# Keys of the second mixer turned once and swapped between partition halves; values projected as features and transposed

## The chip, the cores and the metric

The kernel runs on one core of one Trainium2 chip. The metric is the device time of one execution in microseconds. Three executions of the kernel before took 2218.27, 2221.05 and 2222.43 us; their median, 2221.05 us, is the time before.

## The reference

A network of two blocks on one sequence of 256 positions and width 1024, each block two layers deep, all in fp32. The change lies in the mixer of the second block. There the normalised activations `h` are multiplied by a wide matrix `w_in`, and its columns are split into queries, keys and values of several attention branches, a convolution branch and a pooling branch:

```python
proj = h @ w_in[l]
a_q, a_kv, a_gate, d_q, d_kv, b_in, c_in = jnp.split(proj, splits, axis=-1)
qa = a_q.reshape(bsz, seq, NSA_KV, NSA_R, HEAD_DIM)
kv = a_kv.reshape(bsz, seq, 3, 2, NSA_KV, HEAD_DIM)      # compressed, selected, window
k_cmp = nsa_compress(kv[:, :, 0, 0], ...)                # not rotated
o_slc = nsa_selected_attention(qa_rot, apply_rope(kv[:, :, 1, 0], cos, sin), kv[:, :, 1, 1], sel)
o_win = banded_attention(qa_rot, apply_rope(kv[:, :, 2, 0], cos, sin), kv[:, :, 2, 1], NSA_WINDOW, None)
kvd = d_kv.reshape(bsz, seq, 2, SWA_KV, HEAD_DIM)
o_d = banded_attention(qd, apply_rope(kvd[:, :, 0], cos, sin), kvd[:, :, 1], SWA_WINDOW, swa_sinks[l])

def apply_rope(x, cos, sin):
    x1, x2 = xf[..., : HEAD_DIM // 2], xf[..., HEAD_DIM // 2:]
    return jnp.concatenate([x1 * c - x2 * s, x2 * c + x1 * s], axis=-1)
```

So three branches (selected, window, and the sliding one called d) have keys that are rotated and values that are not. Each has two key heads of 64 features, that is 128 key columns and 128 value columns of `w_in`, and eight query heads, four to each key head.

## The kernel before

Everything is one program for one core. Activations lie with features on partitions and the 256 positions along the free axis. A product with a weight matrix goes in **units** of 1 MB of weights (256 output columns). SyncE loads a unit into one of three slots of a ring (`raw`), ScalarE rounds it to a high part `whi` (`split_hi`, L1287), VectorE computes the low part `wlo` (`split_lo`, L1823), and TensorE multiplies: each product of fp32 accuracy is three matmuls, high by high, high by low, low by high (`mm3`, L615 to L617). A unit is split two units before it is used; ScalarE may overwrite a slot when TensorE is done with the unit that lay there, and SyncE may load into it when its low part is made.

A normal unit is two halves of 128 output columns, each 8 chunks of the depth times three matmuls with 256 moving columns (`project`), 48 matmuls in all. TensorE writes the result into a PSUM bank, and VectorE takes it from there, times the reciprocal norm (`take`).

`mixer2` walks over units 0 to 47 of a layer on TensorE, ScalarE, VectorE and SyncE alike; each engine has its own loop over the same unit numbers, and semaphores tie them. The order inside a unit is written out by hand. The units that matter here are 7, 8 and 9, the **key units** (`K_UNITS`: selected, window, d). The first half of such a unit is the keys (features on partitions). The second half is the values, with positions on partitions as the product with the probabilities needs them: `project_tokens` makes `h` the stationary operand and the weights the moving one, for each of two tiles of 128 positions 8 chunks times three matmuls with 128 moving columns (L702 to L704), again 48.

After unit 8, 9 and 10 TensorE does the **turn** of the keys of the unit before (`TURNS`, kind "k"). The keys of two heads lie on partitions 0 to 63 and 64 to 127. The score products of a pair of query heads use partition half 0 for the one and half 1 for the other, so each key head must stand on both halves. For this the kernel multiplies with a duplicating matrix `dup[g]` and with `rotdup[g]` (duplicate and rotate), four fp32 matmuls of 256 columns (L1054). Each fp32 matmul of this kind leaves two rows in the trace, so a turn has x8. VectorE then makes `kd = dup*cos + rotdup*sin` in three operations of 512 columns (L2302, L2303, L2305). The turn after unit 7 is that of the compressed branch ("cmp"), also four matmuls with `dup`, with eight small VectorE additions (L2314) behind it. The turns after units 2, 3, 11 and 12 rotate queries (L1049).

VectorE's list in the units around this, per unit i: convolution taps (L2436, 5 to 8 of 256 columns), the rest of the turn of unit i-1, the low split for unit i+2, and `take(i)`. From unit 13 on it also has softmax work, at unit 14 the pooling windows (L2407 to L2422), and at unit 16 the low part of the pooled product (L2522). TensorE's product for the pooling (`pool_mix`, L1163) stands behind unit 14; the first transposes of probabilities (L1081) stand behind unit 16. The first score product (`scores(0)`, L1071) stands behind unit 13.

## Time and profile before

| | us |
|---|---|
| median of three executions | 2221.05 |
| the profiled execution | 2222.18 |
| its span in the trace | 2220.4 |
| TensorE busy in the span | 2159.3 (97%) |
| VectorE busy | 1497.8 (67%) |
| ScalarE busy | 1099.7 (50%) |
| mean granted TensorE clock | 0.988 of full |

The span is what the trace covers; 1.8 us of the profiled execution lie outside it. Matmuls overlap, so the duration of one (about 280 ns) is much longer than the distance to the next (0.11 to 0.12 us), and it is the distance that counts in a row of them. The two mixers of the second block lie at about 1120 to 1460 us and 1660 to 1990 us, the two feed-forward stages behind them at about 1480 to 1650 and 2030 to 2200 us.

### The profile page before, as it was taken

How to read it: one execution, taken by the hardware profiler on the slowest of the kernel's cores; microseconds unless marked ns; L12 is line 12 of the kernel's file. 1: busy time of each engine (PE TensorE's matmuls, PEld its weight loads, DVE VectorE, ACT ScalarE, POOL GpSimd, SP SyncE). 2: the span in 40 equal slices, each digit the busy share in tenths (PEclk: the TensorE clock that was granted, in tenths of full speed). 3: DMA queues.
4: the chain of work that ended last, by engine and by line, in shares of the span. 5: the costliest groups of instructions: out<-in, count | busy, mean ns of one | idle time of the engine just before them, and what ended most of it. 6: DMA issues, size and time to landing. Idle time of an engine off the chain costs nothing.

```text
span 2220.4 us, 40876 instructions
## 1 busy us (share of the span) xinstructions
PE 2159.3 (97%) x17966; PEld 2079.9 (94%) x17966; DVE 1497.8 (67%) x1814; ACT 1099.7 (50%) x1336; POOL 127.1 (6%) x116
## 2 busy tenths in 40 slices
PE   8999999999999999999999799999999989999998
PEld 8999999999999999999999698999999879899998
DVE  5556757554655675765568996667766898666775
ACT  5444465444544436544442567455554365655553
POOL 0001000000100100000000000001000000001000
PEclk9999999999999999999999899999999989999999
DMA  7555444555555454455563444346554344354552
GB/s 258 193 187 167 157 143 162 190 190 189 172 186 190 163 164 143 162 190 192 189 191 118 140 142 144 123 163 205 195 180 134 117 146 150 121 171 143 187 184 76
DMA packets 285044, 367.26 MB, mean 165 GB/s; under 512 B 10002, under 2 KB 257730, under 8 KB 284610
## 3 DMA queue, kind: packets, MB, share of 16 engines
q1 hardware_dynamic: 281138, 361.01, 49.3%
q10 hardware_dynamic: 3728, 3.62, 0.5%
q8 instruction: 142, 2.33, 0.4%
q14 instruction: 36, 0.29, 0.0%
HBM read 363.56 MB, written 1.05 MB: 164 GB/s over the span
## 4 chain that ended last, share of the span: by engine, by line
PE 86%; DVE 9%; ACT 3%; issue 1%; DMA 1%; POOL 0%; ACTq 0%; SPq 0%; DVEq 0%
PE ps L615 25%; PE ps L617 25%; PE ps L616 25%; DVE wlo L1823 2%; ACT whi L1287 2%; PE ps L702 1%; PE ps L703 1%; PE ps L704 1%; PE ps L663 1%; DVE sq L2436 1%; PE ps L1054 1%; PE ps L1071 1%; PE ps L1102 1%; PE ps L1081 1%; DVE arena L2112 0%
## 5 line engine op out<-in xcount | busy, mean ns | idle before, releaser
L615 PE MATMUL ps<-hhi,whi 128*128 128x256 f32 x3808 | 1087.7, 286 | 15.5 <-DVE hlo L1829 4.7
L1823 DVE TENSOR_TENSOR wlo<-raw,whi 128x2048 fp32r<-128x2048 f32 (+1 forms) x347 | 781.7, 2254 | 426.6 <-ACT whi L1287 426.5
L616 PE MATMUL ps<-hlo,whi 128*128 128x256 f32 x3808 | 1062.9, 279 | 0.0
L617 PE MATMUL ps<-hhi,wlo 128*128 128x256 f32 x3808 | 1062.7, 279 | 0.0
L1287 ACT ACTIVATE whi<-raw 128x2048 fp32r<-128x2048 f32 (+1 forms) x347 | 652.9, 1884 | 700.6 <-PE ps L617 611.7
L615 PEld LDWEIGHTS ps<-hhi,whi 128*128 128x128 f32 x3808 | 717.4, 188 | 34.3 <-issue 12.9
L616 PEld LDWEIGHTS ps<-hlo,whi 128*128 128x128 f32 x3808 | 717.0, 188 | 6.5 <-issue 6.0
L617 PEld LDWEIGHTS ps<-hhi,wlo 128*128 128x128 f32 x3808 | 720.9, 189 | 0.2
L615 PE MATMUL ps<-hidhi,whi 128*128 128x256 f32 x1056 | 295.5, 280 | 0.3 <-DVE hidlo L2193 0.3
L617 PE MATMUL ps<-hidhi,wlo 128*128 128x256 f32 x1056 | 294.7, 279 | 0.0
L616 PE MATMUL ps<-hidlo,whi 128*128 128x256 f32 x1056 | 294.7, 279 | 0.0
L617 PEld LDWEIGHTS ps<-hidhi,wlo 128*128 128x128 f32 x1056 | 200.4, 190 | 0.0
L615 PEld LDWEIGHTS ps<-hidhi,whi 128*128 128x128 f32 x1056 | 198.5, 188 | 0.9 <-DVE hidlo L2193 0.5
L616 PEld LDWEIGHTS ps<-hidlo,whi 128*128 128x128 f32 x1056 | 198.6, 188 | 0.0
L1365 ACT ACTIVATE arena<-arena 128x512 f32<-128x512 f32 x44 | 27.8, 633 | 176.5 <-DVE arena L1858 176.4
L615 PE MATMUL ps<-brhi,whi 128*128 128x256 f32 x320 | 92.0, 287 | 7.4 <-DVE brlo L2544 6.6
L2436 DVE SCALAR_TENSOR_TENSOR sq<-arena,par,sq 128x256 f32<-128x256 f32 x240 | 98.1, 476 | 0.0
L1780 POOL TENSOR_TENSOR arena<-arena,rstd 128x512 f32<-128x512 f32 x44 | 57.1, 1298 | 629.5 <-ACT arena L1365 603.6
L616 PE MATMUL ps<-brlo,whi 128*128 128x256 f32 x320 | 90.6, 283 | 0.0
L617 PE MATMUL ps<-brhi,wlo 128*128 128x256 f32 x320 | 90.5, 283 | 0.0
L2188 DVE SCALAR_TENSOR_TENSOR arena<-arena,par 128x256 f32<-128x256 f32 x176 | 73.6, 479 | 1.5 <-ACT arena L1549 1.3
L615 PEld LDWEIGHTS ps<-brhi,whi 128*128 128x128 f32 x320 | 62.0, 194 | 9.2 <-issue 7.7
(288 smaller groups left out, 2108.7 us busy)
## 6 DMA issues: line engine op xcount, KB each, us to landing
raw<-in_ffn_w_up SPq DMA_DIRECT2D x88, 1024.0 KB, 5.1
raw<-in_w_in SPq DMA_DIRECT2D x68, 1024.0 KB, 5.2
raw<-in_ffn_w_down SPq DMA_DIRECT2D x66, 1024.0 KB, 4.8
raw<-in_ffn_w_gate SPq DMA_DIRECT2D x43, 1024.0 KB, 5.2
raw<-in_w_gate SPq DMA_DIRECT2D x32, 1024.0 KB, 5.4
raw<-in_w_branch SPq DMA_DIRECT2D x16, 1024.0 KB, 4.9
raw<-in_nsa_cmp_w SPq DMA_DIRECT2D x8, 1024.0 KB, 5.5
raw<-in_w_out SPq DMA_DIRECT2D x6, 1024.0 KB, 4.8
```

The costliest lines, as they stand in the source:

```text
L615: pe.matmul(o, w_hi, m_hi, start=start, stop=False, skip_group_check=True)
L616: pe.matmul(o, w_hi, m_lo, start=False, stop=False, skip_group_check=True)
L617: return pe.matmul(o, w_lo, m_hi, start=False, stop=stop, skip_group_check=True)
L663: last = pe.matmul(bank(2, n * t, n), src[:, chunk, t * P:(t + 1) * P], w, start=first and t == 0, stop=final, skip_group_check=True)
L702: pe.matmul(o[:, t, :], hhi[:, k, tok], whi[:, slot, c:c + n], start=(k == 0), stop=False)
L703: pe.matmul(o[:, t, :], hlo[:, k, tok], whi[:, slot, c:c + n], start=False, stop=False)
L1287: act.activation(whi[:, slot, 0:n], raw[:, slot, 0:n], ACT.Copy).then_inc(hi_ready[slot], 1)
L1365: act.activation(act_out, gate_sb, ACT.Silu).then_inc(act_done, 1)
L1780: pool.tensor_tensor(scaled.rearrange("p (c t) -> p c t", c=2), act_out.rearrange("p (c t) -> p c t", c=2), rstd_over(2), ALU.mult).then_i ...
L1823: dve.tensor_tensor(wlo[:, slot, 0:n], raw[:, slot, 0:n], whi[:, slot, 0:n].bitcast(F32), ALU.subtract) \
L2188: dve.scalar_tensor_tensor(conv2[:, w, c, :], pad2[:, w, c, tap:tap + SEQ], par_col(ch + tap * FCH), conv2[:, w, c, :], ALU.mult, ALU.add) ...
L2436: dve.scalar_tensor_tensor(conv_acc[:, c, :], x, w, conv_acc[:, c, :], ALU.mult, ALU.add) \
```

## The change

In the key units the values are now projected like everything else, features on partitions, and taken together with the keys by one VectorE operation into `ktv`. In the turn TensorE transposes the values of the unit (two transposes of 128 columns into bank 3) and rotates the keys once, by one fp32 matmul of 256 columns into bank 4. ScalarE copies the transposed values out of PSUM to `vt`. VectorE computes `keys*cos + rotated*sin` once, for 256 columns, into `kd[:, k, 0]`. Two DMAs, issued by ScalarE, copy partitions 64 to 127 to 0 to 63 of `kd[:, k, 1]` and the other way round. The score product picks copy 0 or 1 according to whether the key head already lies on the half that the query uses. The compressed branch is as it was. The table of constants of the second block loses `rotdup` (256 of 2178 columns). Three semaphores of the first normalisation are merged into others with the same waits.

```diff
-C2_AT, C2_N = layout([("cos", SEQ), ("sin", SEQ), ("rot", P), ("dup", 2 * P), ("rotdup", 2 * P),
+C2_AT, C2_N = layout([("cos", SEQ), ("sin", SEQ), ("rot", P), ("dup", 2 * P),
...
-        ktmp = view(m2["s"][:, 0:3 * SEQ], k=3, t=SEQ)
-        cmp_kv = view(m2["s"][:, 3 * SEQ:5 * SEQ], v=2, t=SEQ)
+        ktv = view(m2["s"], k=3, v=2, t=SEQ)
+        cmp_kv = ktv[:, 2, :, :]
...
 # TensorE, turn
+                    elif kind == "k":
+                        if k:
+                            pe.wait_ge(v_taken, l * 3 + k)
+                        for t in range(TT):
+                            last = pe.transpose(bank(3, t * P, P), ktv[:, k, 1, t * P:(t + 1) * P], ident)
+                        last.then_inc(v_turned, 1)
+                        last = pe.matmul(bank(4, 0, SEQ), rot2, ktv[:, k, 0, :], start=True, stop=True)
                     else:
-                        for b, m, src in ((3, dup, ktmp[:, k, :]), (4, rotdup, ktmp[:, k, :])) if kind == "k" else \
-                                ((3, dup, cmp_kv[:, 0, :]), (4, dup, cmp_kv[:, 1, :])):
+                        for v in range(2):
                             for g in range(KVH):
-                                last = pe.matmul(bank(b, g * SEQ, SEQ), m[:, g, :], src, start=True, stop=True)
+                                last = pe.matmul(bank(3 + v, g * SEQ, SEQ), dup[:, g, :], cmp_kv[:, v, :], start=True, stop=True)
...
 # TensorE, scores
                     if j == 0:
                         pe.wait_ge(rope2_done, (l + 1) * len(ROPES) - 1)
+                        pe.wait_ge(v_taken, (l + 1) * 3)
+                        pe.wait_ge(k_swapped, (l + 1) * 3 * 32)
...
-                            k = kd[lane, kind, 2 * c // GRP, 0:keys]
+                            k = kd[lane, kind, int(i != 2 * c // GRP), 0:keys]
...
 # TensorE, second half of every unit
-                            if i in K_UNITS:
-                                last = project_tokens(slot, P, P, UC, bank(b, SEQ, SEQ).rearrange("p (t n) -> p t n", t=TT))
-                            else:
-                                last = project(slot, 1, bank(b, SEQ, SEQ))
-                            last.then_inc(used[slot], 1)
+                            project(slot, 1, bank(b, SEQ, SEQ)).then_inc(used[slot], 1)
...
 # ScalarE, per unit
+                    for unit, kind, k in TURNS:
+                        if kind == "k" and unit + 1 == i:
+                            act.wait_ge(v_turned, l * 3 + k + 1)
+                            act.activation(vt[:, k, :, :], bank(3, 0, TT * P).rearrange("p (t n) -> p t n", t=TT), ACT.Copy) \
+                                .then_inc(v_taken, 1)
+                        if kind == "k" and unit + 2 == i:
+                            act.wait_ge(rope2_done, l * len(ROPES) + ROPE_OF_K[k] + 1)
+                            for half in range(2):
+                                act.dma_start(kd[half * DH:(half + 1) * DH, k, 1, :], kd[(1 - half) * DH:(2 - half) * DH, k, 0, :]) \
+                                    .then_inc(k_swapped, 16)
...
 # VectorE, take
-                    if i in K_UNITS:
-                        k = K_UNITS[i]
-                        dve.tensor_tensor(ktmp[:, k, :], bank(bank2_of(f), 0, SEQ), rstd_b, ALU.mult)
-                        dve.tensor_tensor(vt[:, k, :, :], bank(bank2_of(f), SEQ, SEQ).rearrange("p (t n) -> p t n", t=TT),
-                                          rstd_t.unsqueeze(2).broadcast_to([P, TT, P]), ALU.mult).then_inc(taken2, 1)
-                        return
...
+                    elif i in K_UNITS:
+                        dst = ktv[:, K_UNITS[i], :, :]
...
 # VectorE, turn
-                        dve.tensor_tensor(kd[:, k, :, :], two(bank(3)), cos2, ALU.mult)
-                        dve.tensor_tensor(ropes2, two(bank(4)), sin2, ALU.mult).then_inc(rot2_taken, 1)
+                        same, part = kd[:, k, 0, :], ropes2[:, 0, :]
+                        dve.tensor_tensor(same, ktv[:, k, 0, :], cos2[:, 0, :], ALU.mult)
+                        dve.tensor_tensor(part, bank(4, 0, SEQ), sin2[:, 0, :], ALU.mult).then_inc(rot2_taken, 1)
                         dve.wait_ge(rot2_taken, r + 1)
-                        dve.tensor_tensor(kd[:, k, :, :], kd[:, k, :, :], ropes2, ALU.add).then_inc(rope2_done, 1)
+                        dve.tensor_tensor(same, same, part, ALU.add).then_inc(rope2_done, 1)
```

How instructions stand on TensorE where unit 8 of the first layer ends and its turn follows, before (`arena` holds all buffers of a mixer; `consts` the table; `ps` is PSUM):

```order
9424 L702 MATMUL ps<-whi,hhi 128x128
9425 L703 MATMUL ps<-whi,hlo 128x128
9426 L704 MATMUL ps<-wlo,hhi 128x128
9427 L1054 MATMUL ps<-arena,consts 128x256 x4
9428 L615 MATMUL ps<-hhi,whi 128x256
9429 L616 MATMUL ps<-hlo,whi 128x256
```

And the same place after the change (its line numbers are 3 to 8 higher):

```order
9376 L618 MATMUL ps<-hhi,whi 128x256
9377 L619 MATMUL ps<-hlo,whi 128x256
9378 L620 MATMUL ps<-hhi,wlo 128x256
9379 L1057 MATMUL ps<-ident,arena 128x128 x2
9380 L1059 MATMUL ps<-arena,consts 128x256
9381 L618 MATMUL ps<-hhi,whi 128x256
```

The matmuls of 128 columns are gone from the unit's end, and the four fp32 products of the turn have become two transposes and one product. Nothing else of TensorE has moved: the unit, the turn and the next unit follow one another as they did.

ScalarE in units 8 to 15 of the first layer, before:

```order
416 L1287 ACTIVATE whi<-raw 128x2048 x3
417 L1677 ACTIVATE hidhi<-gates 128x480 x2
418 L1287 ACTIVATE whi<-raw 128x2048 x2
419 L1287 ACTIVATE whi<-raw 128x192
420 L1287 ACTIVATE whi<-raw 128x2048 x3
```

After:

```order
417 L1684 ACTIVATE arena<-ps 128x256
418 L1694 ACTIVATE hidhi<-gates 128x480 x2
419 L1294 ACTIVATE whi<-raw 128x2048
420 L1689 DMA arena<-arena 64x256 x2
421 L1684 ACTIVATE arena<-ps 128x256
422 L1294 ACTIVATE whi<-raw 128x2048
423 L1689 DMA arena<-arena 64x256 x2
424 L1684 ACTIVATE arena<-ps 128x256
425 L1294 ACTIVATE whi<-raw 128x192
426 L1689 DMA arena<-arena 64x256 x2
```

The three value copies and the three pairs of swap DMAs stand between the high splits, each behind the split of its own unit. The last pair stands behind the small split (192 columns) for unit 14 and ahead of the split for unit 15.

## Rows read from the trace of the kernel before

**Rows 1.** Units 7 to 12: busy us of PE, PEld, DVE, ACT, POOL; clock, DMA.

```profile
1170.00:1219.00 49.00, 49.00 (x392) 47.45 (x391) 40.42 (x71) 10.64 (x9) 0.00 (x0) 1.00 0.35 108
```

**Rows 2.** Waits of TensorE: total us, times, the longest.

```profile
PE ps L1163 <- DVE gates L2422: 16.9, 2, 8.7
PE ps L1081 <- DVE brlo L2522: 8.8, 2, 5.0
PE ps L615 <- DMA consts<-const_tables: 2.1, 1, 2.1
```

**Rows 3.** The chain that ended last, 1130 to 1330 us: start, us, what.

```profile
1212.21 0.86 PE ps L1049 x2
1218.76 0.69 DVE gates L2281
...
1262.96 0.66 PE ps L1081 x6
```

**Rows 4.** Timeline of TensorE, units 8 and 9: start, us, instruction, x how many.

```profile
1182.01 0.22 PE L702 MATMUL ps<-whi,hhi 128*128 128x128 f32 x1
...
1187.32 1.94 PE L1054 MATMUL ps<-arena,consts 128*128 128x256 f32 x8
1188.91 0.47 PE L615 MATMUL ps<-hhi,whi 128*128 128x256 f32 x1
1189.21 0.28 PE L616 MATMUL ps<-hlo,whi 128*128 128x256 f32 x1
...
1191.92 0.22 PE L702 MATMUL ps<-whi,hhi 128*128 128x128 f32 x1
```

**Rows 5.** The same view of two stretches of the feed-forward stages.

```profile
1520.00:1540.00 20.00, 20.00 (x179) 20.00 (x178) 14.41 (x16) 10.61 (x11) 2.44 (x2) 1.00 0.60 202
2080.00:2100.00 20.00, 20.00 (x173) 20.00 (x172) 13.21 (x16) 11.18 (x11) 2.58 (x2) 1.00 0.62 208
```

**Rows 6.** Timeline of VectorE, units 7 to 12, first layer.

```profile
1173.42 2.28 DVE L1823 TENSOR_TENSOR wlo<-raw,whi 128x2048 fp32r<-128x2048 f32 x1
1177.60 0.42 DVE L2250 TENSOR_TENSOR arena<-ps,rstd 128x256 f32<-128x256 f32 x1 [1.90 <-PE ps L704]
...
1183.27 2.29 DVE L1823 TENSOR_TENSOR wlo<-raw,whi 128x2048 fp32r<-128x2048 f32 x1
...
1197.43 0.42 DVE L2250 TENSOR_TENSOR arena<-ps,rstd 128x256 f32<-128x256 f32 x1 [3.06 <-PE ps L704]
...
1200.08 0.68 DVE L2302 TENSOR_TENSOR arena<-ps,consts 128x512 f32<-128x512 f32 x1
...
1202.01 2.28 DVE L1823 TENSOR_TENSOR wlo<-raw,whi 128x2048 fp32r<-128x2048 f32 x1
1204.21 1.22 DVE L2321 TENSOR_TENSOR hidlo<-gates,hidhi 128x480 fp32r<-128x480 f32 x2
...
1212.24 0.69 DVE L2283 SCALAR_TENSOR_TENSOR arena<-ps,rstd 128x512 f32<-128x512 f32 x1
...
1217.22 0.35 DVE L1823 TENSOR_TENSOR wlo<-raw,whi 128x192 fp32r<-128x192 f32 x1
1218.76 0.69 DVE L2281 TENSOR_TENSOR gates<-ps,rstd 128x512 f32<-128x512 f32 x1 [1.18 <-PE ps L617]
```

**Rows 7.** Timeline of VectorE, the same units, second layer.

```profile
1717.04 2.28 DVE L1823 TENSOR_TENSOR wlo<-raw,whi 128x2048 fp32r<-128x2048 f32 x1
...
1761.82 0.69 DVE L2281 TENSOR_TENSOR gates<-ps,rstd 128x512 f32<-128x512 f32 x1 [0.99 <-PE ps L617]
```

**Rows 8.** Timelines: ScalarE's queue issuing three DMAs; TensorE's first scores in the first layer.

```profile
1114.73 1.69 ACTq L1640 DMA_DIRECT2D arena<-in_nsa_cmp_w  x3
...
1225.16 0.92 PE L1071 MATMUL ps<-arena 64*128 64x256 f32 x8
```

**Rows 9.** DMA issues: queue, count, KB each, median us to landing.

```profile
consts<-const_tables ACTq DMA_DIRECT2D x1, 1089.0 KB, 7.4
...
arena<-in_nsa_cmp_w ACTq DMA_DIRECT2D x6, 64.0 KB, 4.5
```

More of the change, by code:

```diff
@@ L191, in shape_consts @@
     half = (r[:, None] // DH) == np.arange(2)[None, :]
-    c2 = np.concatenate([cos, sin, rot, *dup, *(x @ rot for x in dup), *causal, *window, cmpadd, cmp01, blockdiag, inv, half], 1)
+    c2 = np.concatenate([cos, sin, rot, *dup, *causal, *window, cmpadd, cmp01, blockdiag, inv, half], 1)
     return (np.eye(P, dtype=np.float32), np.ascontiguousarray(c1, np.float32), np.ascontiguousarray(c2, np.float32))
@@ L343, in hybrid_network @@
         rot2 = table(C2_AT, "rot", P)
-        dup, rotdup = (view(table(C2_AT, x, 2 * P), g=KVH, n=P) for x in ("dup", "rotdup"))
+        dup = view(table(C2_AT, "dup", 2 * P), g=KVH, n=P)
         causal, window = (table(C2_AT, x, 3 * P).unsqueeze(1).broadcast_to([P, 2, 3 * P]) for x in ("causal", "window"))
@@ L398, in hybrid_network @@
         x_updated = sem("x_updated")
-        first_sq, first_root, first_rec, first_diag, first_wide, first_kept = (
-            sem(n) for n in ("first_sq", "first_root", "first_rec", "first_diag", "first_wide", "first_kept"))
+        first_sq, first_diag, first_wide, first_kept = (
+            sem(n) for n in ("first_sq", "first_diag", "first_wide", "first_kept"))
         h_hi, h_ready = sem("h_hi"), sem("h_ready")
@@ L422, in hybrid_network @@
             "kcvb_done kcvb_taken sc_scored hid_turned sc_step sc_exp sc_den sc_pt ptc_taken s2_done s2_taken mn2_step p2_done "
-            "den2_step rec2_done p2_normed t2_done pt2_taken pv2_done ob2_hi ob2_ready cg_on c_ready conv_step "
+            "rec2_done p2_normed t2_done pt2_taken pv2_done ob2_hi ob2_ready cg_on c_ready conv_step "
             "ln_mean ln_cent ln_sqd ln_var ln_stdd ln_step silu_done ga_raw ga_tanh ga_on pads pool_step pooled pool_mm "
             "pool_hi pool_lo gates_on br_done gated2 y2_done y2_hi y2_ready").split())
+        v_turned, v_taken = sem("v_turned"), sem("v_taken")
+        k_swapped = sem("k_swapped")
         block = ctx.enter_context(nc.Block())
@@ L808, in first_rstd @@
             def first_rstd():
-                pe.wait_ge(first_diag, 1)
+                pe.wait_ge(first_diag, 2)
                 pe.matmul(bank(3, 0, SEQ), ones, diag.rearrange("p t n -> p (t n)"), start=True, stop=True).then_inc(first_wide, 1)
@@ L1422, in first_norm @@
                 act.wait_ge(first_sq, 2)
[L1423 removed]
+                act.activation(col_std[:, 0:TT], col_tmp[:, 0:TT], ACT.Sqrt, scale=1.0 / D, bias=eps_col).then_inc(first_sq, 1)
             def turned_par():
@@ L1932, in first_norm @@
                 low(7)
-                dve.wait_ge(first_root, 1)
-                dve.reciprocal(col_rec[:, 0:TT], col_std[:, 0:TT]).then_inc(first_rec, 1)
-                dve.wait_ge(first_rec, 1)
+                dve.wait_ge(first_sq, 3)
+                dve.reciprocal(col_rec[:, 0:TT], col_std[:, 0:TT]).then_inc(first_diag, 1)
+                dve.wait_ge(first_diag, 1)
                 widen(col_rec[:, 0:TT], diag).then_inc(first_diag, 1)
```

3 lines of the change are left out of this document (1 added, 2 removed).

## The prediction

> **What bounds the kernel now.** I read the busy times first, for the whole span (TensorE 97%, in the table above) and for the stretch of units 7 to 12: TensorE is busy for 49.00 of 49 us there, VectorE for 40.42, ScalarE for 10.64 [rows 1]. Where a kernel is bound like that, a matmul taken out is worth its distance to the next one, unless TensorE then only waits longer further on. So the second view is the list of TensorE's waits [rows 2]: few, and the two large ones (16.9 and 8.8 us over both layers, two waits each) stand in the second mixer, shortly behind the units that the change touches. The third view, the chain of waits in order of time, tells which engine sets the pace there. Up to 1212 us its long pieces are TensorE's own, the turns among them; at 1218.76, with VectorE's take of unit 12, it goes over to VectorE, and only behind the wait at L1081 do TensorE's turns and transposes come back into it [rows 3]. So units 7 to 12 are TensorE's, units 13 to 16 VectorE's. The change saves TensorE time just ahead of a stretch that VectorE sets. What it is worth depends on how early VectorE can reach the take of unit 12. For that I read VectorE's timeline, with the idle time ahead of a row and what ended it in brackets.
>
> **The values.** In unit 8 the 48 matmuls of 128 columns run from 1182.01 to 1187.32, 5.31 us, 0.111 us each [rows 4]. Half the columns do not cost half the time: 256 columns cost 0.118 us: from 1189.21, the second matmul of unit 9, to its second half at 1191.92 there are 23, 2.71 us. The change puts 24 matmuls of 256 columns there: 24 x 0.118 = 2.83 us. Saved per key unit 2.48 us. The Trainium skill (TensorE: Matmul & The Clock Gate, Back-to-back issue gap) gives N/2.4 + 2.5 ns for an isolated warm matmul, 109 ns for 256 columns, and about 81 ns for a pair of weight load and 128 columns; by it the unit would save only 48 x 0.081 - 24 x 0.109 = 1.3 us, and the time would come out 7 us higher over the six units. The rows have 111 ns for the 128 columns, so I go by them.
>
> **The turn.** Before, eight rows of L1054 take 1.59 us to the start of the next unit at 1188.91, 0.20 us each, and the second matmul of that unit starts 0.30 instead of 0.12 us later: 1.77 us [rows 4]. After: two transposes, at the 0.11 us of six in 0.66 [rows 3], 0.22 us; one fp32 product, two rows of 0.20; the same 0.18 us of change back: 0.80 us. Saved 0.97 us. Together 3.45 us per key unit, 10.3 us for three, if nothing holds TensorE up.
>
> **Can VectorE follow?** A list of VectorE's work after the change, from the row of the low split at 1173.42, which ends 2.20 us later, at 1175.6 (consecutive starts, as at 1202.01 and 1204.21). The take of unit 7, which waited for TensorE, stood at 1177.60; TensorE is now 2.5 us earlier, so 1175.1, and the take of unit 7 starts at once. From there:
> - to the take of unit 8: 1177.60 to 1183.27 plus a split of 2.20, 7.87 us (the two takes of 256 become one of 512; gain counted as nothing);
> - to that of unit 9: take and taps 2.65 (1197.43 to 1200.08), turn, split 2.20. The turn is 1.93 before (1200.08 to 1202.01); each of its three operations goes from 512 to 256 columns, 0.68 to 0.42 us: 1.93 - 0.78 = 1.15. Sum 6.0;
> - to that of unit 10: 6.0 and the 1.2 of L2321, 7.2; to that of unit 11: 6.0;
> - to that of unit 12: 1212.24 to 1217.22 plus the small split 0.35, 5.3.
>
> Sum 32.4 us: VectorE is ready at 1208.0. TensorE is done with unit 12 at 1218.76 - 10.3 = 1208.4 [rows 6]. VectorE arrives 0.4 us ahead; the first layer gets its 10.3 us, with no idle time of VectorE left. Second layer: 1717.04 + 2.20 + 32.4 = 1751.6 against 1761.82 before [rows 7]; here VectorE is last by a hair and the gain is 10.2 us. In between, TensorE needs the take of the unit before last for its bank and that of the last for the turn, each some 5 us ahead of need. From the take of unit 12 on, VectorE's chain is as long as before, and all behind it moves up by what the take moved up. The two large waits keep their size.
>
> **What is added.** Three copies of 256 columns and six DMA issues per layer on ScalarE, the issues 0.56 us each (1.69 for three, [rows 8]). ScalarE is busy for 10.64 of 49 us there [rows 1]; 0.4 and 1.1 us more per unit lie in its idle time. The last swap waits for VectorE's turn in unit 11 (1196.7 + 2.65 + 1.15 = 1200.5) and for the small split behind unit 11's end (1212.2 - 10.3 = 1201.9 [rows 3], plus 0.4), is issued by 1203.4 and lands, by the 4.5 us of the 64 KB loads [rows 9], at 1208. The first scores come at 1225.16 - 10.3 = 1214.9 [rows 8]. With 7 us of slack it costs nothing; beyond 11.5 us from issue to landing the excess would be on the path. The Trainium skill (DMA: Bandwidth & Descriptors, Rules for kernel authors) says that two transfers to disjoint partition halves serialise, which speaks against the pair. Even twice the row's 4.5 us fits.
>
> **The table.** TensorE waits 2.1 us for the second table [rows 2], 1089 KB in 7.4 us [rows 9]. 128 KB less is 0.87 us if all of the 7.4 scales, and 0.36 by the slope from the 64 KB row (2.9 us for 1025 KB). I take 0.6, bounds 0 (something else late by then) and 0.9. The merged semaphores keep their waits: nothing.
>
> **Sum.** 10.3 + 10.2 + 0.6 = 21.1 us. The profiled execution took 2222.18 us: 2201.1. It is 1.1 us above the median of 2221.05, so the forecast is 2200.0 us.
>
> **An unknown of another kind.** At full granted clock (1.00 in both rows) the same projections run at two paces: 179 matmuls in 20 us in the feed-forward stage of the first layer, 173 in that of the second [rows 5], 3.5%. Nothing in the work differs, so the pace seems to depend on how the engines happen to fall into step behind some pause. The change shifts all that follows, so each later stretch may fall the other way. One feed-forward stage of some 150 us is worth 5 us; one stage was fast and one slow, so I expect 0, with some 6 us to each side.
>
> **Rivals.**
> *VectorE does not get narrower.* If 256 columns out of SBUF and PSUM cost the turn as much as 512 (bound from above: 1.93 us), three turns per layer cost 2.3 us more and VectorE is at unit 12 at 1210.3 and 1753.9: gains 8.5 and 7.9, time 2222.2 - 17.0 - 1.1 = 2204; with each link of its list 0.3 us slower by waits on TensorE, 2207. For: it has no slack left. Against: the row of a 256-column take shows 0.42. Chance 10%.
> *The gain is only a longer wait.* If VectorE set the pace already from unit 7, TensorE would arrive early at L1163 and wait 10 us more: 2221. For: the wait there is the largest. Against: VectorE idles 1.90, 3.06 and 1.18 us in units 7 to 12, each time for TensorE [rows 6]. All that stays is its own shortening, 3 us per layer at most, partly. Chance 4%, between 2215 and 2221.
> *Slower: the swap sets the scores.* The first score product waits for all six DMAs of the layer. It decides from the point at which the last lands after 1214.9, and costs more than the change saves when it lands after 1225.2, 22 us from its issue, with TensorE idle at L1071 and VectorE's softmax behind it. At 30 us it would be 8 us late in each layer: 2221 + 16 = 2237. Against: 4.5 us in the row of the same size, queue nearly empty there. The other way to the same place is a fault of the order, ScalarE held by the wait for the turn while TensorE needs a split; by the times above that wait is always over when it is reached. Chance 3%.
>
> **How the numbers follow.** Forecast 83%, at 2200 with its own range 2193 to 2208 (pace +-6, VectorE's list +-1.5); first rival 10%, near 2205, also mostly inside; second 4%; third 3%. A difference under 0.2% (4.4 us) can't be told from none. So faster 93%, same 4%, slower 3%. Range 2193 to 2208.
>
> **What would show it.** TensorE: no matmuls of 128 columns in units 7 to 9; from the end of unit 8's last projection to the second matmul of unit 9 about 0.9 us. TensorE's busy time down by about 20 us, its waits at L1163 and L1081 as before (some 17 and 9). VectorE: its take of unit 12 near 1208 and 1751 less the table's part, idle time ahead of it under 1 us. The swap landing before the scores, no wait for it. Wrong would be: a new wait at the scores or at the first turn, a wait at L1163 longer by more than 2 us, or VectorE's take of unit 12 above 1210.

## The result, and the profile after

| | before | changed |
|---|---|---|
| median, us (executions) | 2219.83 (4) | 2192.95 (4) |
| lowest and highest, us | 2218.27, 2222.43 | 2189.15, 2200.51 |
| the profiled execution, its span | 2222.18, 2220.4 | 2200.51, 2198.7 |
| TensorE busy in the span, us | 2159.3 | 2136.5 |
| mean granted clock | 0.988 | 0.986 |

The ratio is 0.9878, with a 95% interval from 0.9849 to 0.9907. The forecast was 2200.0 with a range from 2193 to 2208: the median lies 7 us below the forecast, just outside the range, while the profiled execution took 2200.51 us. Only the profiled one of the four executions has a trace. So there are two questions: did the change do what the steps said, and where do the other 7 us come from?

First the stretch that was changed. The windows view of units 7 to 12 in the changed kernel (start:end, total, then busy us and number of instructions of PE, PEld, DVE, ACT, POOL, then clock, DMA share, GB/s), to be held against [rows 1]:

```profile
1164.00:1202.00 38.00, 38.00 (x310) 36.68 (x309) 37.60 (x68) 12.03 (x12) 0.00 (x0) 1.00 0.49 150
```

The same units take 38 instead of 49 us. TensorE has some 80 instructions fewer. VectorE, busy for 40.4 of 49 us before, is now busy for 37.6 of 38. Its timeline, units 6 to 12, against [rows 6] (start, us, instruction; an idle time before a row would stand in brackets):

```profile
1163.58 0.69 DVE L2294 TENSOR_TENSOR arena<-ps,rstd 128x512 f32<-128x512 f32 x1 [1.35 <-PE ps L620]
...
1169.73 0.68 DVE L2294 TENSOR_TENSOR arena<-ps,rstd 128x512 f32<-128x512 f32 x1
...
1177.65 0.69 DVE L2294 TENSOR_TENSOR arena<-ps,rstd 128x512 f32<-128x512 f32 x1
1178.26 2.06 DVE L2450 SCALAR_TENSOR_TENSOR sq<-arena,par,sq 128x256 f32<-128x256 f32 x5
1180.23 0.41 DVE L2316 TENSOR_TENSOR arena<-arena,consts 128x256 f32<-128x256 f32 x1
1180.57 0.41 DVE L2317 TENSOR_TENSOR arena<-ps,consts 128x256 f32<-128x256 f32 x1
1181.02 0.42 DVE L2319 TENSOR_TENSOR arena<-arena 128x256 f32<-128x256 f32 x1
1181.36 2.29 DVE L1840 TENSOR_TENSOR wlo<-raw,whi 128x2048 fp32r<-128x2048 f32 x1
...
1201.75 0.69 DVE L2294 TENSOR_TENSOR gates<-ps,rstd 128x512 f32<-128x512 f32 x1
```

From the take of unit 6 to that of unit 12 it is 1201.75 - 1163.58 = 38.17 us; before it was 1218.76 - 1169.47 = 49.29. The first layer gained 11.1 us. In the second layer the two takes stand at 1699.51 and 1737.69, 38.18 us, against 48.73 (1713.09 to 1761.82): 10.6 us. No row after the first has an idle time ahead of it, and the three operations of the turn, of 256 columns each, take 1181.36 - 1180.23 = 1.13 us.

TensorE's timeline at the turn behind unit 8, against [rows 4]:

```profile
1182.42 0.28 PE L620 MATMUL ps<-hhi,wlo 128*128 128x256 f32 x1
1182.53 0.38 PE L1057 MATMUL ps<-ident,arena 128*128 128x128 f32 x2
1182.75 0.60 PE L1059 MATMUL ps<-arena,consts 128*128 128x256 f32 x2
...
1188.65 0.38 PE L1057 MATMUL ps<-ident,arena 128*128 128x128 f32 x2
...
1200.96 0.28 PE L620 MATMUL ps<-hhi,wlo 128*128 128x256 f32 x1
```

One unit with its turn is 1188.65 - 1182.53 = 6.12 us long. The two transposes take 0.22 us to the start of the key rotation. The last row is the end of unit 12: TensorE is done with it at 1201.24, and VectorE takes it at 1201.75, without idle time ahead. So VectorE is the last by 0.5 us. The waits of TensorE, against [rows 2] (what for, total us, times, the longest):

```profile
PE ps L1174 <- DVE gates L2436: 18.0, 2, 9.1
PE ps L1092 <- DVE brlo L2536: 9.0, 2, 4.5
...
PE ps L618 <- DMA consts<-const_tables: 1.7, 1, 1.7
```

They are the waits of before, 16.9, 8.8 and 2.1 us there. The swap, from the list of DMA issues (KB each, median us to landing) and the timelines of ScalarE's queue and of TensorE, against [rows 8, 9]:

```profile
consts<-const_tables ACTq DMA_DIRECT2D x1, 961.0 KB, 7.0
arena<-arena ACTq DMA_DIRECT2D x12, 64.0 KB, 2.0
```

```profile
1195.05 1.12 ACTq L1689 DMA_DIRECT2D arena<-arena  x2
...
1207.49 0.92 PE L1082 MATMUL ps<-arena 64*128 64x256 f32 x8
```

A pair is issued in 1.12 us, and each copy lands 2.0 us behind its issue (the median of twelve; one took 4.4), here by 1198.2 at the latest; the first scores stand at 1207.49, with no wait.

Now the pace. The windows of 20 us in the five long feed-forward stretches behind the first one (columns: total, PE busy and number of matmuls, clock, DMA share, GB/s), of the profiled execution of the changed kernel:

```profile
440.00:460.00 20.00, 20.00 (x172) 1.00 0.56 177
620.00:640.00 20.00, 20.00 (x179) 1.00 0.58 184
1000.00:1020.00 20.00, 20.00 (x178) 1.00 0.64 210
1520.00:1540.00 20.00, 20.00 (x172) 1.00 0.58 189
2060.00:2080.00 20.00, 20.00 (x172) 1.00 0.51 172
```

Both paces of [rows 5] are there, 172 and 179 matmuls in 20 us, at a granted clock of 1.00. From the distances between the starts of projections in the trace: they are 113.3 ns at the fast pace and 117.8 ns at the slow one (4.4 ns apart, unrounded), and nothing between. A stretch of 1340 takes 151.8 or 157.8 us. Before, the five were slow, slow, fast, fast, slow; here slow, fast, fast, slow, slow. The two profiled executions so have the same number of matmuls at the slow pace, some 8000 each, and the 21.7 us between their spans are the change at equal pace.

### The profile page after: what moved, and what is told of

Same layout as the page of the kernel before. It is cut to its first block, busy times and chain, and to the rows that moved or that the text cites. A ratio compares the mean times of both kernels' runs of the same rounds, so it can differ in the third digit from the quotient of the medians.

```text
span 2198.7 us, 40554 instructions
## 1 busy us (share of the span) xinstructions
PE 2136.5 (97%) x17798; PEld 2058.5 (94%) x17798; DVE 1491.7 (68%) x1808; ACT 1100.5 (50%) x1342; POOL 127.1 (6%) x116
## 4 chain that ended last, share of the span: by engine, by line
PE 83%; DVE 12%; ACT 3%; issue 1%; DMA 1%; POOL 0%; SPq 0%; ACTq 0%; DVEq 0%
PE ps L618 25%; PE ps L620 24%; PE ps L619 24%; DVE wlo L1840 3%; DVE sq L2450 2%; ACT whi L1294 2%; PE ps L666 1%; PE ps L705 1%; PE ps L707 1%; PE ps L706 1%; PE ps L1082 1%; PE ps L1092 1%; PE ps L1113 1%; DVE arena L2129 0%; PE ps L877 0%
## 5 line engine op out<-in xcount | busy, mean ns | idle before, releaser
L618 PE MATMUL ps<-hhi,whi 128*128 128x256 f32 x3856 | 1099.8, 285 | 16.4 <-DVE hlo L1846 5.7
L619 PE MATMUL ps<-hlo,whi 128*128 128x256 f32 x3856 | 1075.4, 279 | 0.0
L620 PE MATMUL ps<-hhi,wlo 128*128 128x256 f32 x3856 | 1075.3, 279 | 0.0
L618 PEld LDWEIGHTS ps<-hhi,whi 128*128 128x128 f32 x3856 | 725.3, 188 | 35.3 <-issue 12.6
L619 PEld LDWEIGHTS ps<-hlo,whi 128*128 128x128 f32 x3856 | 726.8, 188 | 6.5 <-issue 6.0
```

Source lines behind the costliest of these rows:

```text
L618: pe.matmul(o, w_hi, m_hi, start=start, stop=False, skip_group_check=True)
L619: pe.matmul(o, w_hi, m_lo, start=False, stop=False, skip_group_check=True)
L620: return pe.matmul(o, w_lo, m_hi, start=False, stop=stop, skip_group_check=True)
```

## The experiments

Times are medians, with the lowest and the highest in brackets; kernels of one group ran on the same chip with the kernel before. The first group was to tell whether the 7 us come from the change or from the pace.

**The changed kernel again, and its parts.** The first is the changed kernel, unchanged. The second has the values of the change, and the keys rotated as before. The third has the keys of the change and the values as before. The fourth has the whole change but the table in its old size.

> The changed kernel once more, unchanged, beside the kernel before. Between VectorE's take of unit 6 and its take of unit 12 the profiles show 49.3 and 48.7 us before and 38.2 and 38.2 us after, 21.7 us less in both layers together. The first series of times says 27 us less. Theory A (the change is worth what its stretch shows, about 21 to 22 us, and the rest is at which of the two paces the long stretches happen to run): the ratio over more runs moves up towards 0.990, single runs of the changed kernel spread over 10 us, and its span follows the number of matmuls at the slow pace. Theory B (the change also saves some 5 us elsewhere, every time): the ratio stays at 0.988 or below, and a second profile shows the 5 us in one place.

> Only the values are projected as features and transposed (into bank 6); the keys are duplicated and rotated by four products as before, no swap. By the forecast's terms each key unit saves 2.5 us for the projection and pays 0.2 for two transposes: 6.9 us per layer between the takes of units 6 and 12, 13.8 us in all, ratio 0.994. Theory B has no other number for it unless the excess belongs to the values: then 0.9915.

```diff
-                        last = pe.matmul(bank(4, 0, SEQ), rot2, ktv[:, k, 0, :], start=True, stop=True)
+                        for b, m in ((3, dup), (4, rotdup)):
+                            for g in range(KVH):
+                                last = pe.matmul(bank(b, g * SEQ, SEQ), m[:, g, :], ktv[:, k, 0, :], start=True, stop=True)
```

> Only the keys: rotated once, swapped by DMA; the values are projected with positions on partitions as before. The turn goes from 1.77 to about 0.5 us: 3.8 us per layer between the takes of units 6 and 12, 7.6 us in all, and 0.5 for the smaller table, ratio 0.996. With theory B and the excess in the keys or the swap: 0.994.

```diff
-                            project(slot, 1, bank(b, SEQ, SEQ)).then_inc(used[slot], 1)
+                            if i in K_UNITS:
+                                last = project_tokens(slot, P, P, UC, bank(b, SEQ, SEQ).rearrange("p (t n) -> p t n", t=TT))
```

> The changed kernel with the table of constants at its old size (the 256 columns of rotdup are loaded and not used). TensorE's wait for the table goes from 1.7 us back to 2.1 us: 0.4 us slower than the changed kernel if the pace falls alike. Theory B with the excess in the table: 5 us slower, ratio 0.990 where the changed kernel beside it has 0.988.

```diff
-C2_AT, C2_N = layout([("cos", SEQ), ("sin", SEQ), ("rot", P), ("dup", 2 * P),
+C2_AT, C2_N = layout([("cos", SEQ), ("sin", SEQ), ("rot", P), ("dup", 2 * P), ("rotdup", 2 * P),
```

| | us | ratio, 95% interval | take of unit 6 to 12, both layers |
|---|---|---|---|
| before | 2214.00 (2199.71 to 2228.46, 31) | | 49.29, 48.73 |
| changed, again | 2194.94 (2186.18 to 2201.39, 9) | 0.9913 (0.9880 to 0.9946) | 38.17, 38.18 |
| values alone | 2200.85 (2190.97 to 2202.91, 10) | 0.9941 (0.9916 to 0.9967) | 42.16, 41.38 |
| keys alone | 2208.92 (2198.87 to 2213.85, 10) | 0.9986 (0.9959 to 1.0012) | 44.86, 44.86 |
| old table | 2191.33 (2181.72 to 2200.34, 9) | 0.9905 (0.9875 to 0.9935) | 38.18, 38.18 |

The kernel before, which in three executions had spread over 4 us, spreads over 29 us in 31. That alone takes the meaning from a gap of 7 us between medians of four. Over the larger number the gain is 19.1 us, not 26.9. In whole times the keys alone can't be told from no change. In the stretch itself the parts can be told apart to half a microsecond: the values give 7.1 and 7.4 us (by the forecast's terms, less the two transposes, (2.48 - 0.22) x 3 = 6.8), the keys 4.4 and 3.9 (the turn without the transposes, (0.97 + 0.22) x 3 = 3.6), and together 11.6 and 11.2, against 11.1 and 10.6 for the two at once: they add up, less what VectorE takes back. The half microsecond between the layers is the pace again: of the 49.29 us before, 203 projections ran at the slow pace, of the 48.73 us 72, and 131 x 4.4 ns = 0.58 us. The changed kernel's 38.17 to 38.18 us, set by VectorE, don't move with it. The table can't be seen in the times (2191.33 with the old, 2194.94 with the new); its wait is 1.8 to 2.1 us in the four profiles with 1089 KB, and 1.0 to 2.2 in the twelve with 961 KB.

The windows of the changed kernel's second profiled execution:

```profile
440.00:460.00 20.00, 20.00 (x172) 1.00 0.61 198
620.00:640.00 20.00, 20.00 (x173) 1.00 0.59 183
1000.00:1020.00 20.00, 20.00 (x179) 1.00 0.57 180
1520.00:1540.00 20.00, 20.00 (x172) 1.00 0.54 177
2060.00:2080.00 20.00, 20.00 (x179) 1.00 0.58 190
```

The second stretch was fast in the first execution and is slow here, the fifth the other way round, with the same instructions. The pace is no property of the kernel. It varies in the five long stretches; of the two shorter ones at the start (26 to 102 us and 107 to 200 us) the first was fast and the second slow in all ten profiles without a product at their start. To compare single executions I take 4.4 ns off the span for each matmul at the slow pace ("corrected span"): 2185.2 us before, 2163.5 and 2161.4 in the two executions after, 21.7 and 23.8 us apart.

**Is VectorE the last?** One more VectorE product of 512 columns behind each key turn.

> The changed kernel with one more VectorE product of 512 columns (about 0.60 us, result unused) behind each of the three key turns of a layer. Theory A (VectorE is the last to arrive at the take of unit 12, with no idle time left from unit 7 on): each of the three is paid in full, 1.8 us per layer, VectorE's take of unit 6 to that of unit 12 takes 38.2 + 1.8 = 40.0 us in both layers, and the span corrected for the pace (span less 4.4 ns for each matmul run at the slow pace) is 3.6 us above the 2161 to 2163 of the changed kernel. Theory B (TensorE still sets these units and VectorE has slack): the distance stays at 38.2 us, below 38.6, and the corrected span within 1 us. The uncorrected time can move by 5 us either way by the pace alone in both theories.

```diff
                         dve.tensor_tensor(same, same, part, ALU.add).then_inc(rope2_done, 1)
+                        dve.tensor_tensor(spare, ktv[:, k, :, :], cos2, ALU.mult)
```

2194.90 us (2190.51 to 2205.99, 5). The takes of units 6 and 12 on VectorE:

```profile
1168.09 0.69 DVE L2294 TENSOR_TENSOR arena<-ps,rstd 128x512 f32<-128x512 f32 x1 [1.14 <-PE ps L620]
...
1208.05 0.68 DVE L2294 TENSOR_TENSOR gates<-ps,rstd 128x512 f32<-128x512 f32 x1
```

39.96 us, and 39.97 (1701.98 to 1741.95) in the second layer: 1.8 us more, each product paid in full. So units 7 to 12 have changed hands, from TensorE to VectorE, and with this change the place gives no more unless VectorE loses work too. The other half of the expectation was not met: the corrected span is 2163.4 us, 0 to 2 us and not 3.6 above the changed kernel's, and so the 3.6 us are seen in the stretch alone.

**Single small instructions between the projections.** Where two executions of one kernel differ, something short must decide. The stretches differ from their surroundings by what passes TensorE between projections, so I put seven kinds of small instruction there.

> The changed kernel with single small TensorE instructions (a product of 1, 64, 512 and 192 columns in bf16, one of 1 and one of 128 columns in fp32, one transpose; results unused) between the projections of units 3, 4, 5, 10, 6, 8 and 9 of the feed-forward stages behind the first. Theory A (the pace is a phase between weight loads and matmuls that is kept until something else than a projection passes TensorE): at some of the places the distance of the following matmuls changes from 117.8 to 113.3 ns or back, always at the same kind of instruction, and it never changes where there is none. Theory B (the pace is given by memory or by something outside of the order of instructions): the pace of each stage stays what it was at its start, through all seven. The instructions themselves cost about 1 us per stage.

```diff
+                    if p == 3 and f:
+                        pe.matmul(bank(5 - odd, 0, 1), zeros[:, 0:P], zeros[:, 0:1], start=True, stop=True, skip_group_check=True)
...
+                    if p == 8 and f:
+                        pe.matmul(bank(5 - odd, 0, P), ones, ones, start=True, stop=True, skip_group_check=True)
```

2196.92 us (one execution). Windows of 10 us in the first of the five stretches, one behind each instruction:

```profile
415.00:425.00 10.00, 10.00 (x87) 1.00 0.51 158
431.00:441.00 10.00, 10.00 (x87) 1.00 0.38 118
448.00:458.00 10.00, 10.00 (x91) 1.00 0.38 123
465.00:475.00 10.00, 10.00 (x90) 1.00 0.45 139
482.00:492.00 10.00, 10.00 (x90) 1.00 0.45 151
513.00:523.00 10.00, 10.00 (x88) 1.00 0.43 145
530.00:540.00 10.00, 10.00 (x87) 1.00 0.45 150
550.00:560.00 10.00, 10.00 (x91) 1.00 0.61 190
```

The first row lies ahead of all seven and the others follow in the order of the expectation's kinds: 1 column, 64, 512 bf16; 1, 128 fp32; transpose; 192 bf16. Slow is 87 or 88, fast 90 or 91. The other four stretches give the same from the second instruction on:

| stretch from | start | 1 | 64 | 512 | 1 fp32 | 128 fp32 | transpose | 192 |
|---|---|---|---|---|---|---|---|---|
| 411 us | slow | slow | fast | fast | fast | slow | slow | fast |
| 598 | fast | slow | fast | fast | fast | slow | slow | fast |
| 963 | slow | fast | fast | fast | fast | slow | slow | fast |
| 1489 | fast | slow | fast | fast | fast | slow | slow | fast |
| 2022 | fast | slow | fast | fast | fast | slow | slow | fast |

The pace changes only at the instructions, and three of them decide it in 5 of 5 stretches: 64 and 192 columns set the fast one, 128 in fp32 the slow one. One column leaves it to chance (it changed the pace in four of five, three times to slow). All this is one execution, each kind at one place of a stretch. The 64 columns, at which the first stretch turns from slow to fast, in TensorE's timeline:

```profile
444.47 0.28 PE L620 MATMUL ps<-hidhi,wlo 128*128 128x256 f32 x1
444.59 0.20 PE L762 MATMUL ps<-zeros 128*128 128x64 bf16 x1
444.63 0.36 PE L618 MATMUL ps<-hhi,whi 128*128 128x256 f32 x1
```

**Fewer waits behind unit 12, and the swap late.** Two experiments on the waits that the change left.

> The changed kernel with ten of VectorE's 124 convolution taps per layer moved: the six of unit 13 and four of the eight of unit 15 go to units 21, 22, 23, 25 and 27. Theory A (from the take of unit 12 on, VectorE's chain sets the time of the pooled product, L1174, and of the probabilities' transposes): ten taps of 0.41 us are 4.1 us off VectorE's chain; TensorE's wait for VectorE at L1174 (9.0 us per layer) and the one at L1092 (4.5) fall by 4 us together per layer, and the corrected span falls by up to 8 us, provided that VectorE isn't late in units 21 to 27. Theory B (the later taps make VectorE late there): waits of TensorE for VectorE's takes or splits come up in units 22 to 28 and the corrected span falls by under 2 us or rises.

```diff
-CONV_TAPS = {7: 6, 8: 5, 9: 5, 10: 5, 11: 5, 12: 6, 13: 6, 15: 8, 16: 8, 17: 8, 18: 8, 19: 6, 20: 6, 21: 6, 22: 6, 23: 5, 24: 7,
-             25: 4, 26: 7, 27: 7}
+CONV_TAPS = {7: 6, 8: 5, 9: 5, 10: 5, 11: 5, 12: 6, 15: 4, 16: 8, 17: 8, 18: 8, 19: 6, 20: 6, 21: 8, 22: 8, 23: 7, 24: 7,
+             25: 7, 26: 7, 27: 8}
```

2196.47 us (2184.13 to 2202.44, 6). The waits:

```profile
PE ps L1174 <- DVE gates L2436: 15.6, 2, 7.8
...
PE ps L1092 <- DVE brlo L2536: 6.6, 2, 3.3
PE ps L1167 <- DVE arena L2409: 3.4, 2, 1.7
```

27.0 us of waits became 22.2 and one of 1.6 became 3.4, so 3 us are left of the 8 at most; corrected span 2157.5. (In the changed kernel's second execution the 27.0 were 28.6, so a good microsecond of this is scatter.) The whole time doesn't show it: this execution had 8843 matmuls at the slow pace, against 7209.

> The changed kernel with all six swaps of a layer issued in ScalarE's turn of unit 14, about 12 us later than the last is issued now. Theory A (landing is 2.0 us behind the issue and the first scores, at 1207.5 us in the first layer, need all six): issue of six takes 3.4 us from about 1207.6, the last lands near 1213, TensorE waits some 5 us at the first scores; the part of it that VectorE's softmax passes on is 2 to 5 us per layer, so the corrected span rises by 4 to 10 us. Theory B (the swaps have more slack than that because VectorE is the last there anyway): TensorE's wait at the scores appears, but the wait at the probabilities' transposes falls by the same amount and the corrected span rises by under 2 us.

```diff
-                        if kind == "k" and unit + 2 == i:
+                        if kind == "k" and i == 14:
```

2210.62 us (2204.81 to 2218.51, 10). The issue on ScalarE's queue, the scores on TensorE, and the list of DMA issues:

```profile
1208.28 3.75 ACTq L1689 DMA_DIRECT2D arena<-arena  x6
...
1216.42 1.19 PE L1082 MATMUL ps<-arena 64*128 64x256 f32 x3 [8.26 <-DMA arena<-arena]
```

```profile
arena<-arena ACTq DMA_DIRECT2D x12, 64.0 KB, 4.9
```

The third rival's mechanism is real: once the swaps land late, TensorE waits at the scores and all behind it moves (the pooled product 8.6 us, 1228.72 against 1220.13 with unit 12 taken at the same time; 8.1 us in the second layer, counted from the take of unit 12). Both theories priced it too low. Six in a row land 4.9 us behind their issue in the median, not 2.0 as in pairs, the last 1216.4 - 1212.0 = 4.4 us behind the end of the issues; and nothing is made up for: 15.7 us over the changed kernel's 2194.94 (another chip), and as much over the wide-turn version's 2194.90 on the same chip, as the third rival's rule of one for one has it (8 us late in each layer, 16 us).

**Setting the pace.** One product of 192 columns behind the wide product that starts each long feed-forward stretch (7 places in the trace, not the 8 of the expectations), in the changed kernel and in the one before; with 128 fp32 columns in its stead; and with the moved taps.

> The changed kernel with one bf16 product of 192 columns (about 0.1 us, result unused) behind the wide product at the start of each feed-forward stretch, 8 in all. Theory A (the pace is a phase that such a product sets to the fast one, as in all five stages of the run with the single instructions): all seven long stretches of projections run at 113.3 ns, also the ones that were slow, the same in every execution; the span is 2162 (corrected for the pace) + 15 (slow matmuls that stay in the mixers, some 3470 at 4.4 ns) + 1 = 2178 us, the median 2180 and the times of several runs lie within 6 us. Theory B (the seven stages of that run fell fast by chance, or the product sets the phase only from the slow one or only further inside): the mix of paces stays, median 2195 with 10 to 15 us between runs.

```diff
                 pe.matmul(bank(b), ones, xT[:, 0:2, :], start=True, stop=True, skip_group_check=True)
+                pe.matmul(bank(b, 0, 192), zeros[:, 0:P], zeros[:, 0:192], start=True, stop=True, skip_group_check=True)
```

> As the run with the 192 columns, but with one fp32 product of 128 columns in that place (about 0.3 us, result unused). Theory A: all long stretches run at 117.8 ns; 7748 matmuls x 4.4 ns = 34 us over the version with the 192 columns, and 1 to 2 us for the products: span about 2213, median 2215, though the change is in it in full. Theory B: median 2195 as for the changed kernel.

```diff
+                pe.matmul(bank(b, 0, P), ones, ones, start=True, stop=True, skip_group_check=True)
```

> The kernel before the change with the same bf16 product of 192 columns at the same 8 places. Theory A: the pace is equal in it and in the changed kernel with that product, so that the difference of the two is the change alone: span 2185 + 15 + 1 = 2201, median 2203, 21 to 23 us over the changed kernel with it, with a spread of few us. Theory B: the change is worth more or less than 21 us where the pace is equal, and the median is outside 2199 to 2207.

> The 192-column products and the ten moved taps together in the changed kernel. Theory A (moved taps take some 4 to 5 us of TensorE's waits in the second mixer away, as in the corrected spans 2157.5 against 2161 to 2163): median 4 to 6 us below the version with the products alone, at 2175. Theory B (that difference was scatter): equal within 1.5 us.

| | us | stretches fast |
|---|---|---|
| before | 2221.32 (2206.64 to 2226.89, 11) | |
| before, 192 columns | 2202.49 (2200.42 to 2207.65, 6) | 7 of 7 |
| changed, 192 columns | 2182.89 (2180.46 to 2184.90, 5) | 7 of 7 |
| changed, 128 fp32 columns | 2183.79 (2180.26 to 2185.00, 4) | 7 of 7 |
| changed, 192 columns, moved taps | 2179.11 (2175.06 to 2181.49, 5) | 7 of 7 |

The product works: from it on all seven stretches are fast in each profile, and the times of one kernel lie within 4.4 us in the changed one. It is worth 19 us in the kernel before, on the same chip, and some 12 in the changed one (2194.94 on another chip, 2182.89). With the pace equal in the seven stretches, the change itself can be measured at last: the means are 2202.98 and 2182.57 us, 20.4 us apart, 95% interval 17.2 to 23.6, ratio 0.991 (0.989 to 0.992). The sum had 21.1. The traces say where. From the 192-column product ahead of the first layer's second mixer to the one behind it, it is 534.83 us before (952.39 to 1487.22) and 526.51 in the changed kernel (952.58 to 1479.09); in the second layer it is 543.21 us (to 2030.43) and 533.25 (to 2012.34). No other piece differs by more than 0.8 us. Within the mixers the pace was not set: the changed kernel's profile has some 700 matmuls more at the slow pace, 3 us against it. The simple rule of Theory A failed in one point: 128 fp32 columns set the slow pace between projections and the fast one behind the wide product. What a small product sets depends on its place; what in the place decides was not tried. The moved taps gave 3.8 us, just under the 4 to 6 expected (the means are 3.4 us apart, 95% interval 0 to 6.8, so hardly clear of the scatter), and this is the fastest version measured: 0.9819 of the kernel before (0.9792 to 0.9846).

**The slow pace on purpose, and the mixers.**

> The changed kernel with the 192-column products, and in the last five feed-forward stretches one fp32 product of 128 columns more (about 0.3 us, result unused), ahead of the third pair's projections, where it stands between projections as in the run with the single instructions. Theory A (a small product between projections sets the pace, this kind the slow one; in the run with it behind the wide product it stood in other company): each of the five stretches changes from 113.3 to 117.8 ns there and stays so, some 1195 matmuls in three and 1150 in two, 5885 x 4.4 ns = 25.9 us, and 1.5 us for the products: median 2183 + 27 = 2210. Theory B (the position in the feed-forward stretch or the fp32 kind has nothing to do with the pace, the slow units of that run came by chance): 2184 to 2186.

```diff
+                    if p == 3 and f:
+                        pe.matmul(bank(5 - odd, 0, P), ones, ones, start=True, stop=True, skip_group_check=True)
```

2203.49 us (2200.41 to 2206.87, 9). Windows as above:

```profile
440.00:460.00 20.00, 20.00 (x172) 1.00 0.58 190
...
2060.00:2080.00 20.00, 20.00 (x172) 1.00 0.57 189
```

All five are slow from the product on, 5884 matmuls. So the pace can be set to either side, at equal work: 20.6 us between the two versions' medians (on two chips), 17.4 between their profiled spans. That is 6 to 10 less than the 27 expected. The traces show where it went: the second layer's second mixer, from the end of one stretch to the start of the next, takes 387.0 us where fast projections run ahead of it (1625.8 to 2012.8, the 192 columns) and 383.3 where slow ones do. Its first waits, in the version with the 192 columns and in the changed kernel (where that stretch was slow):

```profile
1636.00:1646.00 10.00, 7.36 (x36) 0.87 0.36 104
1646.00:1656.00 10.00, 10.00 (x73) 0.79 0.11 22
```

```profile
1650.00:1660.00 10.00, 7.66 (x54) 1.00 0.28 81
1660.00:1670.00 10.00, 10.00 (x89) 1.00 0.34 105
```

With the fast stretch ahead, the granted clock is 0.79 there over 10 us: for part of them it stands at the lower of its two levels, 1.2 GHz, and for the rest at 2.4. With the slow one it stays at 1.00. In both TensorE has waited some 2 us just before (2.35 us with the 192 columns, 2.13 in the version with the slow pace). The first mixer shows the same at 1105 to 1115 us (0.83). Some 3 us per layer are given back so, and the mean granted clock of the whole span is 0.987 against 0.991. It is a tendency and no rule. Of all profiles but that of the single instructions, 15 in number, the clock fell in the second layer's mixer in all 10 with a fast stretch ahead, and in 1 of 5 with a slow one (the changed kernel's second execution). In the first layer's mixer it fell in 4 of 13 with a fast one, and in none of 2 with a slow one. Why it falls in one case and not in the other was not tried. For the corrected spans it means that 4.4 ns per slow matmul is too much: over these two versions, some 5800 slow matmuls apart, it is 17.4 us, 3.0 ns each. An execution with many slow matmuls, as that of the moved taps, looks better by it than it is.

> The version with the 192-column products and the moved taps, and one bf16 product of 64 columns (some 0.05 us) ahead of each projection unit of both mixers. Theory A (the short product sets the fast pace there too): most of the 3204 matmuls that still run at the slow pace go to the fast one, at 4.4 ns some 10 to 14 us less, against 70 x 0.05 = 3.5 us for the products, and part of it is lost in waits for VectorE: median 2171 to 2176 against 2179. Theory B (within the mixers the pace is set by the transposes and score products between units, after the short product): 2180 to 2184.

```diff
+                            pe.matmul(bank(b, 0, 64), zeros[:, 0:P], zeros[:, 0:64], start=True, stop=True, skip_group_check=True)
                             project(slot, 0, bank(b, 0, SEQ))
```

2180.65 us (2180.11 to 2180.88, 5), against 2179.11 on another chip without them: no gain. The slow matmuls fell from 3204 to 1802, by 1400 x 4.4 ns = 6 us, and the 84 products took it back: at most places one moves the next projections by some 0.11 us, not 0.05, some 7 us in all. TensorE's waits at the pooled product and at the transposes are nearly as without them (15.6 and 6.8 us, against 15.6 and 6.6).

## Why the prediction was wrong in its number and right in all steps but one

- *What bounds the kernel.* Right. TensorE set units 7 to 12, VectorE the stretch behind; the gain appears in full up to the take of unit 12, and the two large waits kept their size (27.0 us against 25.7).
- *Values, turn.* Right. Forecast 10.3 and 10.2 us per layer, measured 11.1 and 10.6, of which half a microsecond in the first layer is pace. The unit with its turn takes 6.12 us; the forecast had 5.66 + 0.80 = 6.46 at the slow pace, and 24 x 2 x 0.1133 = 5.44 plus 0.68 is what was run, so the turn was sized 0.1 too high. The values alone gave 7.1 and 7.4 us for three units, with their transposes paid. By the Trainium skill (TensorE: Matmul & The Clock Gate, Back-to-back issue gap) a unit's values would have saved 1.3 us, an estimate from its 81 ns for 128 columns and 109 ns for 256; the rows of this case (111 ns) and the values alone decide against it here.
- *Can VectorE follow.* Right in its list: 32.4 us were listed from the take of unit 7, 1201.75 - 1169.73 = 32.0 were measured, with no idle time, and the wide-turn run shows that it has none to spare. The order of the two was not as said: VectorE was to arrive 0.4 us ahead of TensorE in the first layer and came 0.5 us behind it, because TensorE was quicker than listed (the turns, and most of its projections there at the fast pace). The first rival (VectorE not narrower) fell with the turn of 1.13 us.
- *The swap.* Right that it is hidden; 2.0 us to landing in pairs instead of the 4.5 of the nearest row. By the Trainium skill (DMA: Bandwidth & Descriptors, Rules for kernel authors) transfers to disjoint partition halves serialise; a pair's 2.0 us leaves little room for that to matter, and no run here moved one half alone. The third rival's price (late us for late us, in each layer) was borne out by the late swap: 8.6 and 8.1 us.
- *The table.* 0.6 was taken. 0.4 us of its wait went (2.1 to 1.7), within the scatter of that wait (1.0 to 2.2 us in twelve profiles with the small table), so no run shows the term.
- *The gain is only a longer wait.* Fell: the waits grew by 1.3 us, the time fell by 20.
- *The pace: the step that failed.* The sum (21.1 us) was right, 20.4 measured with the pace equal, 17.2 to 23.6. What was mis-sized is the term "0, with some 6 us to each side". One long stretch is worth 6.0 us and I let one change sides. There are five such, each falling anew in every execution: the kernel before ran from 2199.7 to 2228.5 us. The base itself, three times within 4 us, agreed so by luck, and it lay high: the later medians are 2214.0 over 31 executions, 2217.4 over 18, 2221.3 over 11 and 2211.3 over 14, on four chips, and their mean over all 74 is 2214.5. From 2221.05 the right sum lands at 2200.0, from 2214.5 it lands at 2193.4, where the result was. So the "0" failed too, as a base of three executions doesn't stand for the middle of the pace. The profiled executions, with 8000 slow matmuls each, differed by the sum; that the other three of the changed kernel (2189 to 2196 us) had fewer is concluded from the later runs and wasn't seen. Whether the chips differ as well was not tested. The range should have been some 15 us to each side, and lower in its middle.

## What to carry to other kernels

Read how far VectorE is from being last before taking work from TensorE: here a slack forecast at 0.4 us came out as VectorE 0.5 us behind, which decided whether 10 us per layer were real, and the next microsecond is no longer TensorE's. Count the matmuls per window in several long stretches of the same work; if two numbers come up at the same granted clock, the time of one execution carries that lottery, and a few executions of before are no base. A small product at the start of each stretch may fix it, and then small changes can be measured.

## What the hardware showed that was not expected

- Two paces of the same fp32r projections at a granted clock of 1.00: 113.3 and 117.8 ns per matmul of 256 columns, held for up to 1340 matmuls through all their waits and loads. They differ between executions of the same kernel, change only at another kind of instruction, and one bf16 product of 64 or 192 columns (0.20 and 0.26 us long, overlapped) set the fast one between projections in five of five places. What in TensorE keeps it was not found.
- Behind a stretch at the fast pace the granted clock fell, around a short wait of TensorE, in 14 of 23 places (to 0.79 over 10 us in one), behind a slow one in 1 of 7.
- A copy of 64 KB within SBUF lands 2.0 us after its issue in a pair, and 4.9 in a burst of six (medians of twelve).
